# Third mixer: one product for queries and their swapped part, key part copied by GpSimd, query statistics between the keys' products

## The reference, cut to what matters

```python
def mla_attention(proj, cos, sin, q_a_norm, w_uq, kv_a_norm, w_ukv, q_norm, k_norm):
    c_q = rms_norm(proj[..., OFF_CQ:OFF_CKV], q_a_norm)        # 256 columns
    c_kv = rms_norm(proj[..., OFF_CKV:OFF_KR], kv_a_norm)      # 128 columns
    k_rope = proj[..., OFF_KR:IN_COLS_2]                       # 32 columns, shared by all heads
    q = (c_q @ w_uq).reshape(B_, S_, 8, 96)
    kv = (c_kv @ w_ukv).reshape(B_, S_, 8, 64 + 64)
    k_nope, v = kv[..., :64], kv[..., 64:]
    k = concatenate([k_nope, broadcast(k_rope)], -1)           # 96 a head
    q = rms_norm(q, q_norm); k = rms_norm(k, k_norm)
    q = concatenate([q[..., :64], apply_rope(q[..., 64:], cos, sin)], -1)
    k = concatenate([k[..., :64], apply_rope(k[..., 64:], cos, sin)], -1)
    ...                                                        # softmax attention, scale 96 ** -0.5
```

## Time and profile before

| | |
|---|---|
| median of 3 runs | 1545.95 us |
| lowest, highest | 1545.14, 1545.99 us |
| the profiled execution | 1537.43 us, span 1535.3 us |
| TensorE busy | 1439.9 us (94% of the span) |
| VectorE busy | 1124.1 us (73%) |
| ScalarE busy | 705.1 us (46%) |
| GpSimd busy | 19.3 us (1%), 16 instructions |
| mean granted TensorE clock | 0.979 |

### The profile page before, as it was taken

How to read it: one execution, slowest core, us unless ns; L and a number is a source line. 1 busy time by engine, 2 the same in 40 slices (tenths; PEclk the granted TensorE clock), 3 DMA queues, 4 the chain that set the end, 5 groups by cost and what they waited for, 6 DMA issues and landing times.

```text
span 1535.3 us, 26554 instructions
## 1 busy us (share of the span) xinstructions
PE 1439.9 (94%) x10992; PEld 1349.6 (88%) x10992; DVE 1124.1 (73%) x1849; ACT 705.1 (46%) x1126; POOL 19.3 (1%) x16
## 2 busy tenths in 40 slices
PE   1999999999999989999999999999999879899998
PEld 1999998788999989999898689999976759799998
DVE  6888988867777788887667766565692766677776
ACT  2434445444343453334445344343544855554543
POOL 0000000000000000010000000000000120000000
PEclk8999999999999999999999999999999979999999
DMA  9986865156777548657333146654312203344541
GB/s 391 415 351 249 339 244 221 55 202 249 283 296 283 224 199 329 283 210 325 143 137 111 34 162 231 230 210 179 130 77 96 110 15 136 125 165 176 196 175 73
DMA packets 32327, 309.29 MB, mean 201 GB/s; under 512 B 3496, under 2 KB 5800, under 8 KB 7504
## 3 DMA queue, kind: packets, MB, share of 16 engines
q1 hardware_dynamic: 32208, 307.60, 52.0%
HBM read 306.53 MB, written 1.06 MB: 200 GB/s over the span
## 4 chain that ended last, share of the span: by engine, by line
PE 83%; DVE 10%; issue 3%; ACT 2%; DMA 2%; SPq 0%; DVEq 0%; ACTq 0%
PE bank L642 13%; PE bank L646 13%; PE bank L643 13%; PE bank L781 12%; PE bank L697 6%; PE bank L699 6%; PE bank L704 6%; DVE WL L1662 2%; PE bank L612 2%; PE bank L658 2%; DMA PR<-in_stream 1%; PE bank L861 1%; PE bank L686 1%; PE bank L850 1%; DVE tmp L1680 1%
## 5 line engine op out<-in xcount | busy, mean ns | idle before, releaser
L1662 DVE TENSOR_TENSOR WL<-ring,WH 128x1024 fp32r<-128x1024 f32 x420 | 504.1, 1226 | 51.3 <-ACT WH L1163 49.1
L1163 ACT ACTIVATE WH<-ring 128x1024 fp32r<-128x1024 f32 x420 | 429.6, 1053 | 135.2 <-PE bank L781 52.6
L642 PE MATMUL bank<-XH,WH 128*128 128x256 f32 x1680 | 410.1, 283 | 1.4 <-ACT WH L1163 1.4
L643 PE MATMUL bank<-XL,WH 128*128 128x256 f32 x1680 | 407.8, 281 | 0.0
L642 PEld LDWEIGHTS bank<-XH,WH 128*128 128x128 f32 x1680 | 316.2, 188 | 7.6 <-issue 6.0
L643 PEld LDWEIGHTS bank<-XL,WH 128*128 128x128 f32 x1680 | 316.2, 188 | 1.0 <-issue 1.0
L646 PE MATMUL bank<-XH,WL 128*128 128x256 f32 x1680 | 233.8, 282 | 1.0 <-DVE WL L1662 1.0
L646 PEld LDWEIGHTS bank<-XH,WL 128*128 128x128 f32 x1680 | 214.0, 188 | 1.2 <-DVE WL L1662 1.2
L1237 ACT ACTIVATE SG<-bank 128x256 f32<-128x256 f32 x88 | 33.8, 384 | 377.0 <-PE bank L646 363.5
L697 PE MATMUL bank<-GH,WH 128*128 128x256 f32 x840 | 202.6, 279 | 0.7 <-ACT WH L1163 0.7
L699 PE MATMUL bank<-GL,WH 128*128 128x256 f32 x840 | 202.5, 279 | 0.0
(11 more groups left out here) (306 smaller groups left out, 1698.8 us busy)
## 6 DMA issues: line engine op xcount, KB each, us to landing
ring<-in_stream SPq DMA_DIRECT2D x133, 1536.0 KB, 6.6
scr<-in_stream SPq DMA_DIRECT2D x15, 1536.0 KB, 10.8
PR<-in_stream SPq DMA_DIRECT2D x15, 1536.0 KB, 8.3
att<-in_stream SPq DMA_DIRECT2D x15, 1536.0 KB, 10.1
ring<-in_stream SPq DMA_DIRECT2D x8, 1024.0 KB, 5.0
ring<-in_stream SPq DMA_DIRECT2D x11, 512.0 KB, 3.6
kf_mix<-in_stream SPq DMA_DIRECT2D x2, 1536.0 KB, 16.0
con<-in_consts SPq DMA_DIRECT2D x1, 2000.0 KB, 19.7
```

Source lines behind the costliest of these rows:

```text
L642: pe.matmul(o, part(WH, u, k), XH[:, k, :], start=(k == 0), stop=False)
L643: pe.matmul(o, part(WH, u, k), XL[:, k, :], start=False, stop=False)
L1163: act.activation(part_all(WH, u), raw(u), ACT.Copy).then_inc(*mark("high", u))
L1662: dve.tensor_tensor(part_all(WL, u), raw(u), part_all(WH, u).bitcast(F32), ALU.subtract)\
```

## The change

The exchanged rotary weights are laid out behind each head's 96 columns, so that one product of 128 columns writes queries to partitions 0 to 95 and the exchanged part to 96 to 127 of the same bank. The tables `mq_swap` and `inv` get rows 96 to 127 accordingly (the angles were computed on all 128 partitions before). The identity products of the keys are gone; GpSimd copies `kr` into rows 64 to 95 of the eight keys, six after `kr_turned`, two after `q_product(3)`, since these lie where the queries' input was, and VectorE waits for them before the keys are scaled. Both value products use bank 7 one after the other: the first stands before the keys with the c_q statistics, the second behind them; ScalarE copies them in pairs 0 and 3. The query statistics of pair p stand behind key pair p. In the third layer's FFN chunk 20 does its own low pass.

```diff
--- before.py
+++ after.py
@@ -673,6 +673,14 @@
 
+                    if c == NFF - 1 and f == 4:
+                        pe.wait_ge(*at(*low_of(u)))
+                        for m in range(KD):
+                            for w, x in ((WH, GH), (WH, GL), (WL, GH)):
+                                last = pe.matmul(out(m), part(w, u, m), x[:, c % 2, :], start=False, stop=(w is WL),
+                                                 skip_group_check=True)
+                            last.then_inc(*mark("ffn_out", f, m))
+                        return
                     if c == NFF - 1:
@@ -697,7 +705,7 @@
                         pe.matmul(out(m), part(WH, u, m), GL[:, c % 2, :], start=False, stop=False, skip_group_check=True)
-                    if c == NFF - 2:
+                    if c == NFF - 2 and f < 4:
                         return
@@ -977,8 +985,7 @@
             m = slot(("mla", 0))
-            uq = m[:, 0:1536].rearrange("p (k h n) -> p k h n", k=2, h=8)
-            uq_swapped = m[:, 1536:2048].rearrange("p (k h n) -> p k h n", k=2, h=8)
+            uq = m[:, 0:2048].rearrange("p (k h n) -> p k h n", k=2, h=8)
             uk = m[:, 2048:2560].rearrange("p (h n) -> p h n", h=8)
@@ -992,35 +999,30 @@
                 take(4 + p % 2, "q_turned", p)
-                take(6 + p % 2, "q_turned", p)
                 if p == 0:
...
                     for k in range(2):
-                        pe.matmul(bank[4 + p % 2][0:96, cols], uq[:, k, 2 * p + i, :], PR[:, 8 + k, body], start=(k == 0), stop=(k == 1))
-                    for k in range(2):
-                        last = pe.matmul(bank[6 + p % 2][64:96, cols], uq_swapped[:, k, 2 * p + i, :], PR[:, 8 + k, body],
-                                         start=(k == 0), stop=(k == 1))
+                        last = pe.matmul(bank[4 + p % 2][:, cols], uq[:, k, 2 * p + i, :], PR[:, 8 + k, body], start=(k == 0),
+                                         stop=(k == 1))
                 last.then_inc(*mark("q_product", p))
...
                     pe.wait_ge(*at("normed", "ckv", 0))
-                    pe.wait_ge(*at("kr_turned"))
                 for i in range(2):
                     cols = slice(i * S, (i + 1) * S)
-                    pe.matmul(bank[4 + p % 2][0:64, cols], uk[:, 2 * p + i, :], lat[:, 2, :], start=True, stop=True)
-                    last = pe.matmul(bank[4 + p % 2][64:96, cols], ident[64:96, 64:96], kr, start=True, stop=True)
+                    last = pe.matmul(bank[4 + p % 2][0:64, cols], uk[:, 2 * p + i, :], lat[:, 2, :], start=True, stop=True)
                 last.then_inc(*mark("k_product", p))
 
-            def values():
-                for t in range(2):
-                    take(6 + t, "v_copied", t)
-                    pe.matmul(bank[6 + t], lat[:, 2, t * P:(t + 1) * P], uv, start=True, stop=True)\
-                        .then_inc(*mark("v_product", t))
+            def values(t):
+                take(7, "v_copied", t)
+                if t == 0:
+                    pe.wait_ge(*at("normed", "ckv", 0))
+                pe.matmul(bank[7], lat[:, 2, t * P:(t + 1) * P], uv, start=True, stop=True).then_inc(*mark("v_product", t))
 
@@ -1030,14 +1032,15 @@
 
-            def q_stats():
-
-                pe.wait_ge(*at("q_squared", 3))
+            def q_stats(p):
+
+                pe.wait_ge(*at("q_squared", p))
                 for t in range(2):
-                    for h in range(8):
+                    for h in (2 * p, 2 * p + 1):
                         last = pe.matmul(bank[6][:, 8 * t + h:8 * t + h + 1], SQ[0:96, h, t * P:(t + 1) * P], ones[0:96, 0:1],
                                          start=True, stop=True)
-                last.then_inc(*mark("q_stat"))
+                if p == 3:
+                    last.then_inc(*mark("q_stat"))
 
@@ -1100,13 +1103,14 @@
                 lru_products(1)
+                values(0)
+                cq_stats()
                 for p in range(4):
                     k_pair(p)
-                values()
+                    q_stats(p)
+                values(1)
                 unit("win2", passes, 10)
-                cq_stats()
                 k_sums()
-                q_stats()
                 unit("win2", passes, 11)
@@ -1503,11 +1507,12 @@
                     act.activation(k_sq[p][0:64], pair(p, 64), ACT.Square).then_inc(*mark("k_squared", p))
-                    act.activation(k96_pairs[p], pair(p, 96), ACT.Copy, scale=prm("mk_nope", rows=96)).then_inc(*mark("k_copied", p))
+                    act.activation(k96_pairs[p][0:64], pair(p, 64), ACT.Copy, scale=prm("mk_nope", rows=64)).then_inc(*mark("k_copied", p))
                     rated(ACT.Tanh, 0, p, LRU[0]["A"][:, p, :], "lru_tanh")
-                for t in range(2):
-                    act.wait_ge(*at("v_product", t))
-                    act.activation(V[:, t, :], bank[6 + t], ACT.Copy).then_inc(*mark("v_copied", t))
+                    if p in (0, 3):
+                        t = p // 3
+                        act.wait_ge(*at("v_product", t))
+                        act.activation(V[:, t, :], bank[7], ACT.Copy).then_inc(*mark("v_copied", t))
 
@@ -1625,6 +1630,13 @@
 
+                    pool.wait_ge(*at("kr_turned"))
+                    for h in range(8):
+                        if h == 6:
+                            pool.wait_ge(*at("q_product", 3))
+                        ins = pool.tensor_copy(k96_pairs[h // 2][64:96, h % 2, :], kr)
+                        if h % 2 == 1:
+                            ins.then_inc(*mark("kr_copied", h // 2))
                     for d in range(2):
@@ -2154,10 +2166,10 @@
                 dve.wait_ge(*at("q_squared", p))
-                gs = par[64:96, PARAM["mq_swap"][0]:PARAM["mq_swap"][0] + 1]
+                gs = par[96:P, PARAM["mq_swap"][0]:PARAM["mq_swap"][0] + 1]
                 for i in range(2):
                     cols = slice(i * S, (i + 1) * S)
-                    dve.scalar_tensor_tensor(SG[64:96, i, :], bank[6 + p % 2][64:96, cols], gs, mrope[64:96, 1, :], ALU.mult, ALU.mult)
+                    dve.scalar_tensor_tensor(SG[64:96, i, :], bank[4 + p % 2][96:P, cols], gs, mrope[96:P, 1, :], ALU.mult, ALU.mult)
                     ins = dve.scalar_tensor_tensor(q96[2 * p + i], bank[4 + p % 2][0:96, cols], prm("mq_norm", rows=96), mrope[0:96, 0, :],
@@ -2198,6 +2210,7 @@
             for p in range(4):
+                dve.wait_ge(*at("kr_copied", p))
                 dve.wait_ge(*at("head_spread", "mk", 2 * p + 1))
@@ -2371,12 +2384,12 @@
         g = f[src][0]
-        put_p(name, np.concatenate([g[:64], np.roll(g[64:], 16)])[:, None])
+        put_p(name, np.concatenate([g[:64], np.roll(g[64:], 16), np.roll(g[64:], 16)])[:, None])
     put_p("mk_nope", np.concatenate([f["mla_k_norm_2"][0, :64], np.ones(32, np.float32)])[:, None])
...
     inv = np.float32(10000.0) ** (-np.arange(0, 32, 2, dtype=np.float32) / np.float32(32))
-    put_p("inv", np.concatenate([np.zeros(64, np.float32), -inv, inv])[:, None])
+    put_p("inv", np.concatenate([np.zeros(64, np.float32), -inv, inv, -inv, inv])[:, None])
     con, bi, fi = constants()
@@ -2422,7 +2435,8 @@
     swapped = np.roll(uq.reshape(P, 2, 8, 96)[:, :, :, 64:], 16, 3)
-    blocks["mla", 0] = np.concatenate([uq, swapped.reshape(P, -1), ukv[:, :, :64].reshape(P, -1), ukv[:, :, 64:].reshape(P, -1)], 1)
+    uq = np.concatenate([uq.reshape(P, 2, 8, 96), swapped], 3)
+    blocks["mla", 0] = np.concatenate([uq.reshape(P, -1), ukv[:, :, :64].reshape(P, -1), ukv[:, :, 64:].reshape(P, -1)], 1)
     proj("wout2", f["w_out_2"][0])
...
```

## The result

| | before | after |
|---|---|---|
| median, of six executions each | 1545.55 us | 1532.95 us |
| lowest to highest | 1541.27 to 1550.83 | 1532.19 to 1539.42 |
| the profiled execution | 1537.43 (span 1535.3) | 1532.53 (span 1530.4) |
| mean granted clock of it | 0.979 | 0.978 |

The two medians stand 12.6 us apart, the two profiled executions 4.9.

A forecast was written before the change was run, and what follows sets the result against it. Third mixer bound by VectorE until 1155.3 us, then mostly TensorE. Keys 4.4, statistics and unit 11 4.2, idle clock -1.7, keys' clock -0.9, GpSimd -1.4, end 1.2: 5.8 off 1545.95 gives 1540.1, range 1535.6 to 1543.8.

The forecast's parts named there:

- the last line of the sum: Whole kernel: the 5.8 us gain taken off the runs' median of 1545.95, 8.5 above the profiled execution, giving 1540.1.
- Queries at nothing: Third mixer's query pairs: 8 us less TensorE work from merging counts as nothing, hidden behind VectorE's 97% busy time.
- Idle clock: Gate products and keys after TensorE's some 6 us stand: lower clock loses 1.7 us, bounds 0 and 3.4.
- Keys: Keys' products: the eight identity products leave TensorE's chain, 4.4 us gained, 3.9 if following products pace slower.
- Statistics: Query statistics among the keys, and unit 11: higher clock gains 2.7 + 1.5 = 4.2 us.
- Keys' clock: Key pairs with statistics between them: a low stretch might come, 0.9 us lost, bounds 0 and 3.4.
- GpSimd: VectorE's stage before the gates: eight key copies contend for memory, 1.4 us lost, bounds 0 and 5.8.
- The rival of a stopped VectorE: GpSimd's copies stop VectorE between 1127.7 and 1155.3 us; 6.4 slower, 1552.4 us; chance 0.05.
- The end: Last FFN: chunk 20's low products move into TensorE's 2.47 us stand, 1.2 us gained, bounds 0.4 and 2.1.
- The bad end: Whole kernel: all terms at their bad bounds together give 8 us slower.

The follow-up runs named there:

- queries_two: Changed kernel with queries and exchanged part as two products again, in two banks; 1535.87 us, ratio 0.9952 to the kernel before.
- only_queries: Kernel before with the merged query product alone; 1545.33 us, ratio 1.0011 to the kernel before.
- only_keys: Kernel before with GpSimd's copies instead of the keys' identity products; 1540.56 us, ratio 0.9975 to the kernel before.
- keys_identity: Changed kernel with the keys' identity products back on TensorE and no GpSimd copies; 1548.97 us, ratio 1.0029 to the kernel before.
- filled: Changed kernel with unit 9, first value product, statistics and first key pair moved into TensorE's two stands; 1529.14 us, ratio 0.9908 to the kernel before.
- before_again: Kernel before, run again with no edit; 1544.16 us, ratio 0.9999 to the kernel before.
- after_again: Changed kernel, run again with no edit; 1537.15 us, ratio 0.9959 to the kernel before.
- end_old: Changed kernel with the last FFN's end as before; 1537.65 us, ratio 0.9969 to the kernel before.

## Why the prediction was wrong, and what of it held

**The step that failed** is the last line of the sum: "The runs' median is 1545.95, 8.5 above that execution, and I take the gain off it". It took the 8.5 between a median of three and one execution for a fixed amount that the changed kernel would keep, and gave the spread of the executions no term and no width in the range. The gain that I took off came out right in size: 5.8 forecast, 5.7 measured in the part that the change touches. The level was not. A median of three of these runs is drawn from two groups 6 us apart, and most of their difference lies in the 1127 us ahead of the change. The forecast of 1540.1 lies above after's mean of 1536.0 by 4.1; of this 2.1 is the first median standing above before's own mean (1545.95 against 1543.8), and the other 2.0 is the pooled 7.9 against 5.8. After's mean lies just inside the range of 1535.6 to 1543.8; the first result's 1532.95 lies 3.0 below it, by the draw of its six. A range of 8 us for a median of a few executions that spread over 14 had no room for this.

**By terms**, from the profiles (mean of four each, where not said):

| | forecast | measured |
|---|---|---|
| first query product to the fifth gate product | -1.4 | -0.8 |
| 24 gate products | -1.7 | -1.9 |
| behind them to k_spread | 4.4 + 4.2 - 0.9 = 7.7 | 6.2; 7.8 in the two profiles shown |
| k_spread and attention | 0 | 1.7 |
| later, to the last convolution | 0 | -0.5 |
| the end | 1.2 | 0.95 |
| sum | 5.8 | 5.7 |

*Queries at nothing*: held (queries_two; only_queries even loses). TensorE stood not once but twice, as the working said, 4.30 us for q_turned(0) and 5.4 for ScalarE.

*Up to the fifth gate product*: in the two profiles shown 0.85 longer. VectorE's own stretch, from kr_turned to the last low, is 0.25 longer; 0.6 lies ahead of it, as the first query product starts 0.3 earlier and kr_turned ends 0.3 later, which I followed no further.

*Idle clock*: the size came out, the cause is not the merged queries alone. Three of the four profiles of after have 7.13 us for the 24 gate products, 1.68 over the 5.45 of all four of before, and the one shown 7.93. But queries_two (stand 1.92) and only_keys (1.92), with two query products, have 7.13 too, and so has keys_identity (4.47), with merged queries and no copies. Before, with a stand of 1.51, is the only one of these that has neither the merged queries nor the copies. Either brings the loss; both together cost no more than one of them in three profiles of four. What makes the clock fall behind 1.92 us there, and not in filled behind 3.07, is open.

*Keys*: L1018 and L1040 of four pairs take 8.0 us, of which the keys 4.0 instead of 8.96: 4.9 gained, 0.5 more than forecast, since the key products that now follow each other pace at 0.25 instead of 0.29.

*Statistics*: mis-sized twice over. Twelve starts in a microsecond was a wrong reading: a stretch counts the instructions that reach into it at both ends. Eight L1040 take 0.98 us, 32 3.92, not 2.7; 1.5 gained, not 2.7, against the profile that was read. And that profile's 5.38 was one of two levels. Before's four profiles have 5.38, 3.66, 5.10 and 3.66, and so over four the term is 0.5; this is before_again's:
```profile
1189.40 3.66 PE bank L1038 x32
```
The weight loads may set their pace, which no run tests: in only_keys' block one is under way through all of the 3.66 us. A 96x128 load has a median of 192 ns, a 128x128 one 188. The Trainium skill, "TensorE: Matmul & The Clock Gate", section "LDWEIGHTS (loading the stationary operand)", says that a load's time goes by its columns and not its rows; the trace agrees. Unit 11: 3.04, 1.4 gained where 1.5 was forecast.

*Keys' clock*: forecast 0.9 lost as a low stretch that might come. In two of four profiles it came, a little later than expected. After_again, the second value product and unit 10:
```profile
1183.11 1.45 PE bank L1025 x2
1184.56 3.93 PE bank L789 x24
```
against 0.97 and 2.84: 1.6 lost, 0.8 on average. Before had its own there, in the statistics, in two of four. With the same order of keys and statistics, queries_two and end_old met a low stretch of 6.8 us that began in the last key pair, so the clock of the keys is not safe at 1.00.

*GpSimd*: 1.4 forecast, 0.25 measured in the profile shown and 0.1 in the other three; 0.4 where the queries are two products. The rate of loss was read from long operations that covered VectorE's; the copies here are short (0.40 undisturbed), 32 partitions high, and four ran beside the reciprocal. The rival of a stopped VectorE fell with it. The 1.7 of clock that came with the copies in only_keys is not in this term; it is the idle clock's.

*The end*: 0.95 on average, near the 1.2 forecast, but bounded by the stores' issues, which the forecast left out.

*Attention*: 1.7 not forecast. k_spread took 3.62, 3.62, 3.62 and 3.97 against 3.62, 4.65, 4.65 and 4.84, which is 0.7 of it; low stretches fall elsewhere once the work before them has moved. That it is this, and not a better order of the work, is read from the clock and was not tested alone.

*The bad end*: "all bad ones 8 slower" doesn't follow from the bounds given. With them the sum is 3.9 + 4.2 - 3.4 - 3.4 - 5.8 + 0.4, 4.1 slower; 8 needs the statistics at nothing, for which no bound was given.

**Open.** 7.9 over all executions and 5.7 in the profiles agree within their uncertainty. Whether the 2.2 between them is real, the runs don't settle: no code ahead of the query products was changed, and the shares of the two groups are alike. Why one execution has 34 us of low clock ahead of the change and the next 61 wasn't found. That errors of terms cancelled (over four profiles: statistics 2.2 too good, GpSimd 1.2 too bad, keys 0.5 and attention 1.7 not counted) is luck.

## What to carry to other kernels

Split the profile at the first changed instruction and compare what lies behind it; a median of a few executions says less of a 0.5% change than that does, and a range for such a median must hold the spread of the executions as well as the terms. A product that is merged in a stage that waits for another engine buys idle time and a free bank, but no time by itself: only_queries lost with it, filled, which put other work into the time and the freed banks, gained 9 us. And test each half of a change by itself before laying a lost clock to one of them: here either half brought the same loss. Where small products are thinned out (32 rows, one column), look at the granted clock of the stage before counting instructions.

## What of the hardware was not expected

- The granted clock stays at 0.50 for 15 us although TensorE is busy 15.20 of 15.20, when 32-column identity products and one-column products are mixed (keys_identity, one profile; its median of 12 executions is 12 us above after_again's). With the identity products gone the same order holds 1.00 in after's four profiles, and has 6.8 us at 0.50 at its end in queries_two and end_old.
- The same program spreads over 1537.1 to 1551.0 us, with 34 to 61 us of low clock ahead of one point in its code. From 275 to 300 us TensorE is busy 22.25 of 25.00 us in an execution at clock 1.00 and 22.26 in one at 0.86.
- A stand of 1.92 us was followed by 1.7 us of lost clock in two kernels, and stands of 1.87 and 3.07 by none in a third (filled).
- SyncE issues a store of 128 KB every 0.4 to 0.5 us, slower than VectorE adds what it stores (0.35 us apart).
- A copy of 32x256 float32 takes GpSimd 0.40 us, and eight of them in VectorE's busiest stage cost it 0.1 to 0.4.
- An instruction with one output column costs as much TensorE time (0.114 to 0.122 us) as a unit's with 256 (0.118), and half as much as one with 256 on plain float32 operands (0.227 in the gate products before).
